# A new order for attention and projections in a one-core transformer layer: first tiles attended between quarters of the projections

## The reference

```python
h = rms_norm(x, g_attn); proj = h @ w_in        # aq 512, ak 64, av 64, iq 512, ik 64, iw 8, bq 512, bk 512, bv 512
# per-head RMSNorm (not for iq) and partial rotary on q and k heads
# group A: score = sum_h relu(iq_h . ik) * iw_h ; keep the top 128 keys of each query ; softmax attention, 8 heads, one k/v
# group B: 4 heads, two softmax maps each: (p1 - lam * p2) @ v, then RMSNorm over each head
# all masks are causal in chunks of 64 tokens
x = x + concat(y_a, y_b) @ w_o
h2 = rms_norm(x, g_ffn); logits = h2 @ w_router + b_router ; top 4 of 32 experts, softmax gates
x = x + sum over experts of gate * (clamped SwiGLU(h2 @ w_gu[e] + b_gu[e]) @ w_down[e] + b_down[e])
```

## Time and profile before

| | us |
|---|---|
| median of 3 runs (lowest, highest) | 1586.6 (1585.97, 1587.24) |
| the profiled execution, its own time | 1583.88 |
| its span from first to last instruction | 1582.1 |
| PE busy | 1475.2 (93%) |
| DVE busy | 1315.8 (83%) |
| ACT busy | 1104.1 (70%) |
| first expert matmul starts | 414.9 |
| PE busy from 500 us to the end | 1068.2 of 1082.1 |

### The profile page before, as it was taken

One profiled execution on the slowest core, in us unless ns is written; L12 is line 12 of the kernel. 1 busy time (PEld: TensorE's weight loads), 2 busy tenths in 40 slices (PEclk: granted clock), 3 DMA queues, 4 the chain that ended last, 5 costly groups with the idle time before them and its releaser, 6 DMA issues.

```text
span 1582.1 us, 18695 instructions
## 1 busy us (share of the span) xinstructions
PE 1475.2 (93%) x7098; PEld 1214.9 (77%) x7098; DVE 1315.8 (83%) x1274; ACT 1104.1 (70%) x1188; POOL 297.4 (19%) x160
## 2 busy tenths in 40 slices
PE   6888858998799999999999999999999999999996
PEld 5766646777577888888888888888888888888885
DVE  5668856554869999999999999999999999998994
ACT  5543454354567878888878878888878878888773
POOL 1644311001112111211112111211111111121101
PEclk9999968799799999999999999999999999999998
DMA  6311010115799999999999999999999999999991
GB/s 193 94 54 54 14 54 27 41 41 203 295 298 358 372 360 367 370 368 367 377 367 373 375 358 364 368 374 368 371 371 372 375 358 364 363 373 360 378 365 42
DMA packets 99244, 448.66 MB, mean 284 GB/s; under 512 B 18368, under 2 KB 19520, under 8 KB 66304
## 3 DMA queue, kind: packets, MB, share of 16 engines
q1 hardware_dynamic: 87264, 428.39, 70.2%
q0 software_dynamic: 9792, 18.90, 5.0%
q10 hardware_dynamic: 2080, 0.01, 0.1%
HBM read 440.95 MB, written 23.07 MB: 293 GB/s over the span
## 4 chain that ended last, share of the span: by engine, by line
PE 84%; DVE 9%; ACT 3%; issue 2%; DMA 0%; POOL 0%; SPq 0%; ACTq 0%; POOLq 0%; DVEq 0%
PE ps L1738 66%; PE ps L1530 2%; PE ps L1537 2%; PE ps L1532 2%; PE ps L1531 2%; PE ps L1748 2%; PE ps L1707 2%; PE ps L1699 2%; PE ps L1618 1%; DVE work L1240 1%; DVE top L1239 1%; DVE rp L1197 1%; DVE ss L1176 1%; PE ps L1648 1%; ACT W L875 1%
## 5 line engine op out<-in xcount | busy, mean ns | idle before, releaser
L653 DVE TENSOR_TENSOR whl<-wraw,whl 128x2048 fp32r<-128x2048 f32 x384 | 865.6, 2288 | 87.7 <-ACT whl L648 83.5
L648 ACT ACTIVATE whl<-wraw 128x2048 fp32r<-128x2048 f32 x384 | 733.1, 1918 | 206.6 <-PE ps L1738 206.4
L1738 PE MATMUL ps<-whl,xT 128*128 128x512 f32 x3120 | 732.2, 392 | 3.0 <-DVE xT L1438 1.7
L1738 PEld LDWEIGHTS ps<-whl,xT 128*128 128x128 f32 x3120 | 582.5, 188 | 124.0 <-issue 2.4
L1738 PE MATMUL ps<-whl,aT 128*128 128x512 f32 x1488 | 346.7, 392 | 0.0
L1738 PEld LDWEIGHTS ps<-whl,aT 128*128 128x128 f32 x1488 | 276.9, 188 | 57.1 <-DVE whl L653 0.3
L821 POOL DMA_INDIRECT out_dram<-ysb,idx x32 | 99.7, 3116 | 451.7 <-ACT ysb L1079 451.7
L812 POOL DMA_INDIRECT xg<-h_rows,idx x32 | 89.7, 2803 | 473.9 <-DVE idx L1426 470.8
L1530 PE MATMUL ps<-W,HT 128*128 128x512 f32 (+1 forms) x184 | 72.0, 392 | 1.7 <-DVE HT L1152 1.7
L1531 PE MATMUL ps<-W,HT 128*128 128x512 f32 (+1 forms) x184 | 70.0, 381 | 0.0
L1532 PE MATMUL ps<-W,HT 128*128 128x512 f32 (+1 forms) x184 | 69.7, 379 | 0.0
(11 more groups left out here) (233 smaller groups left out, 1452.2 us busy)
## 6 DMA issues: line engine op xcount, KB each, us to landing
wraw<-in_w_gu_dram SPq DMA_DIRECT2D x256, 1024.0 KB, 8.1
wraw<-in_w_down_dram SPq DMA_DIRECT2D x128, 1024.0 KB, 7.2
WR<-in_w_in_dram SPq DMA_DIRECT2D x20, 512.0 KB, 3.6
WR<-in_w_o_dram SPq DMA_DIRECT2D x8, 512.0 KB, 3.7
xs<-in_x_dram SPq DMA_DIRECT2D x4, 512.0 KB, 5.9
WR<-in_x_dram SPq DMA_DIRECT2D x4, 512.0 KB, 4.4
out_dram<-WR SPq DMA_DIRECT2D x4, 512.0 KB, 2.7
h_rows<-WR SPq DMA_DIRECT2D x4, 512.0 KB, 2.9
```

The lines of the kernel that those rows point to most:

```text
L648: act.activation(whl[:, n % HL, 0, :], wraw[n % RAW], ACT.Copy).then_inc(chunk_hi, 1)
L653: eng.tensor_tensor(whl[:, n % HL, 1, :], wraw[n % RAW], whl[:, n % HL, 0, :].bitcast(F32), ALU.subtract).then_inc(chunk_lo, 1)
L1738: ins = pe.matmul(bank, a[x_][j], w[:, b, j, 512 * q:512 * q + 512], start=c == NG and j == 0 and n == 0, stop=last and j == nj - 1 and n ...
```

## The change

The chunks are reordered to iq, kvi, aq, bq, bk, bv. A projection becomes four steps of two 128-row blocks (`PARTS`), and between them stand index scores (from stage 8 on, one a quarter), search rounds, and `ATTEND_AT[s]` units of attention. Units are renumbered by `unit(n)`: 0 to 7 are A of tile 0, 8 to 15 A of tile 1, 16 to 23 B of tile 0, 24 to 31 B of tile 1, then tiles 2 and 3 as before. 24 units fall into stages 14 to 22 (`ATTEND_AT`). Heads of bk are split and turned one stage later than others. w_o's splits stand one to a unit at 24 to 31; tile 3's 16 search rounds at units 32 to 47. The table `LATE` places the rest: output projections at units 37 to 44, 46 to 53, 55 to 62, and from 69; routers at 48, 57, 66 and 80 (before: output projections at 21, 37, 53, 69, and routers at 32, 48, 64, 80, each t at 16 units from the last).

The router's product goes to a transpose bank instead of ACC, so `out_proj` waits for `x1_ok` instead of the logits. A results of tiles 0 and 1 have buffers of their own (`yA`), B results of tile 1 use bank OA and another half of y, `work` and `maskA` are packed, and the waits follow the new order. With the last score, the list ends

```diff
 CHUNKS = [("iq", [(O_IQ, 512)]), ("kvi", [(O_IK, 72), (O_AK, 128)]), ("aq", [(O_AQ, 512)]),
-          ("bv", [(O_BV, 512)]), ("bq", [(O_BQ, 512)]), ("bk", [(O_BK, 512)])]
+          ("bq", [(O_BQ, 512)]), ("bk", [(O_BK, 512)]), ("bv", [(O_BV, 512)])]
-AHEAD = 5
+PARTS = 4
+ATTEND_AT = {14: 4, 15: 4, 16: 3, 17: 3, 18: 2, 20: 2, 21: 3, 22: 3}
...
+def unit(n):
+
+    if n < 16:
+        return n // 8, 8 + n % 8
+    if n < 32:
+        return (n - 16) // 8, n % 8
+    return n // 16, n % 16
...
+LATE = {11: [("mix_a", 0)], 19: [("mix_a", 1)],
+        34: [("mix_b", 0)], 35: [("mix_norm", 0)], 36: [("mix_b", 1), ("turn_y", 0)], 38: [("mix_norm", 1)],
+        43: [("mix_b", 2)], 45: [("mix_norm", 2), ("turn_y", 1)], 51: [("mix_a", 2)], 54: [("turn_y", 2)],
+        59: [("mix_b", 3)], 61: [("mix_norm", 3)], 67: [("mix_a", 3)], 68: [("turn_y", 3)]}
+for _t, _n in enumerate((37, 46, 55, 69)):
+    for _k in range(KD):
+        LATE.setdefault(_n + _k, []).append(("out_proj", _t, _k))
+    for _d, _kind in ((8, "post"), (9, "turn_x1"), (9, "post_mean"), (10, "post_norm"), (11, "route")):
+        LATE.setdefault(_n + _d, []).append((_kind, _t))
...
     def attend(n):
...
-            if t >= 1 and j == 7:
+            if t >= 1 and n in (8, 16 * t + 7):
                 while search and search[0][1] <= t:
                     plan.append(search.pop(0))
                 plan.append(("mask", t))
             plan.append(("score", n))
-            if t >= 1:
-                next_search(n >= 22 and n % 16 >= 6)
-        if pieces and n % 2:
+        if n >= 24 and pieces:
             plan.append(pieces.pop(0))
         if product_of(n - 1) and product_of(n - 1)[0] == "B":
             plan.append(("combine", product_of(n - 1)))
+        if n >= 32:
+            next_search(1)
...
+        plan.extend(LATE.get(n, []))
...
-        if s < n_items:
-            plan.append(("proj", s))
-        if s >= 10:
-            for _ in range(4):
-                if scores:
-                    plan.append(scores.pop(0))
-            if s < n_items:
-                next_search(3)
-        if s >= n_items:
-
-            for _ in range(AHEAD):
+        fill = ATTEND_AT.get(s, 0)
+        for q in range(PARTS):
+            if s < n_items:
+                plan.append(("proj", s, q))
+            if s >= first_kv + 5 and scores and ("turn_heads", first_kv + scores[0][1]) in plan:
+                plan.append(scores.pop(0))
+            if q < fill:
                 attend(attended.pop(0))
+            if s < n_items and q < (3 if s < 16 else 2):
+                next_search(1)
...
@@ SP
-            sp.wait_ge(values_ok, HB + HA)
+            sp.wait_ge(values_ok, values_no("B", 0, HB - 1))
             sp.dma_start(GF, bc(g_ffn)).then_inc(gf_in, 16)
...
@@ DVE, mix_a
-                    dve.wait_ge(values_ok, (HB + HA) * (t + 1))
+                    dve.wait_ge(values_ok, values_no("A", t, HA - 1))
...
@@ DVE, route
-                    dve.wait_ge(logit_ps, t + 1)
-                    dve.scalar_tensor_tensor(out=lg[:, t, :], in0=ps[:, ACC, 0:E], scalar=tss[:, 2:3], in1=brt,
-                                             op0=ALU.mult, op1=ALU.add).then_inc(logit_ok, 1)
-                    dve.wait_ge(logit_ok, t + 1)
+                    dve.wait_ge(turned, through(st))
+                    g = TURN[st]
+                    dve.scalar_tensor_tensor(out=lg[:, t, :], in0=tbank(g)[:, 0:E], scalar=tss[:, 2:3], in1=brt,
+                                             op0=ALU.mult, op1=ALU.add).then_inc(turn_read[g % 2], 1)
...
@@ PE, out_proj and route
-                        if t >= 1:
-                            pe.wait_ge(logit_ok, t)
+                        after(pe, x1_ok, t)
...
+                    g = TURN[st]
+                    wait_bank(pe, g)
                     for k in range(KD):
-                        ins = pe.matmul(ps[:, ACC, 0:E], x1T[:, k, :], wrt[:, k, :], start=(k == 0),
+                        ins = pe.matmul(tbank(g)[:, 0:E], x1T[:, k, :], wrt[:, k, :], start=(k == 0),
                                         stop=(k == KD - 1))
-                    ins.then_inc(logit_ps, 1)
+                    ins.then_inc(turned, 1)
```

More of the change, by code:

```diff
@@ L77, in keys_of, with product_of @@
     return P * (t + 1)
+def unit(n):
[4 more added lines that the diff above has]
+    return n // 16, n % 16
+UNITS = 16 * T
+NO = {unit(n): n for n in range(UNITS)}
+def product_of(n):
+    if not 0 <= n < UNITS:
+        return None
+    t, j = unit(n)
+    if j < 8:
+        return ("B", t, j // 2) if j % 2 else None
+    return ("A", t, j - 8)
+LATE = {11: [("mix_a", 0)], 19: [("mix_a", 1)],
[7 more added lines that the diff above has]
+        LATE.setdefault(_n + _d, []).append((_kind, _t))
 def make_plan():
@@ L93, in next_search @@
                 plan.append(search.pop(0))
[L97 to L108, removed]
     def attend(n):
-        if n == len(units) + 5:
+        if n == UNITS + 5:
             plan.append(("biases",))
-        if n < len(units):
-            t, j = units[n]
-            if t >= 1 and j == 7:
+        if n < UNITS:
+            t, j = unit(n)
+            if t >= 1 and n in (8, 16 * t + 7):
                 while search and search[0][1] <= t:
@@ L129, in attend @@
             plan.append(("values", product_of(n - 3)))
[L130 to L139, removed]
+        plan.extend(LATE.get(n, []))
+    attended = list(range(max(LATE) + 1))
     n_items = len(ITEMS)
+    first_kv = ITEM_NO[(CH["kvi"], 0)]
     for s in range(n_items + 3):
@@ L199 @@
 PROD = number(("turn_p",))
+COMBO = number(("combine",))
+REL_PRODS = 2 * HA + HB
 HEADED = [u for u in range(len(ITEMS)) if has_heads(u)]
@@ L585, in combo_no, with values_no, pv_bank @@
         def combo_no(pr):
-            return HB * pr[1] + pr[2] + 1
+            return COMBO[("combine", pr)] + 1
+        def values_no(which, t, h):
+            return PROD[("turn_p", (which, t, h))] + 1
+        def pv_bank(which, t):
+            return OA if which == "A" or t == 1 else OB
         def is0(r):
@@ L690, in _ @@
                 if t >= 1:
-                    sp.wait_ge(logit_ps, t)
+                    sp.wait_ge(turned, through(("route", t - 1)))
                 if t == T - 1:
@@ L1222, in _ @@
                     v, w = SCORE[st], keys_of(t)
-                    dst = work[:, t - 1, 0:w]
+                    dst = work[t]
                     dve.wait_ge(score_read, v + 1)
@@ L1547, in _ @@
                 elif kind == "proj":
-                    u = st[1]
+                    _, u, part = st
                     c, t = ITEMS[u]
-                    if u == 0:
+                    if u == 0 and part == 0:
                         wait_turns(pe, KD)
-                    if u >= 2:
+                    if u >= 2 and part == 0:
                         pe.wait_ge(raw_ok, u - 1)
                     dst = ps[:, ACC + u % 2, 0:WIDTH[c]]
-                    for k in range(KD):
+                    for k in range(KD // PARTS * part, KD // PARTS * (part + 1)):
                         if k % 2 == 0:
@@ L1578, in _ @@
                     n, v = st[1], SCORE[st]
-                    t, j = n // 16, n % 16
+                    t, j = unit(n)
                     w = keys_of(t)
-                    if j == 0:
-                        wait_turns(pe, through(("turn_heads", ITEM_NO[(WO - 1, t)])))
+                    if j % 8 == 0:
+                        wait_turns(pe, through(("turn_heads", ITEM_NO[(CH["bk" if j == 0 else "aq"], t)])))
                     pe.wait_ge(score_read, v - 1)
@@ L1594, in _ @@
                             pe.wait_ge(mask_ok, t)
-                        pe.matmul(dst, identb, maskA[:, t, 0:w], start=False, stop=False)
+                        pe.matmul(dst, identb, maskA[t], start=False, stop=False)
                     pe.matmul(dst, q, keys[1], start=False, stop=True).then_inc(score_ps, 1)
```

143 lines of the change are left out of this document (90 added, 53 removed).

## The result

The changed kernel takes 1599.09 us (median of 4 runs, 1596.39 to 1599.65) against 1586.92 us (4 runs, 1585.97 to 1589.15) for the kernel before beside it: ratio 1.0065, 95% interval 1.0048 to 1.0083. It is slower, by 0.65%; forecast were 1573 us and a range of 1556 to 1589.

The account below looks back on a forecast made before the run. DVE was taken to bound the projections with head work and tile 2, PE the bv projections and tile 3. Last maximum -16.6 us plus tail +3.0 gave -13.6, so 1573 us, range 1556 to 1589.

Parts of the forecast that it names:

- Stages 14 to 18: Projections 14 to 18 with 16 attention units between quarters: DVE bounds, 53.2 us, the units otherwise hidden behind DVE.
- To stage 10: Projections before stage 10, with tile 1's index scores: half of 3.9 us of DVE score passes hidden; group 10 starts near 80.3.
- Stages 10 to 13: Projections 10 to 13 with head work, searches and index scores: DVE bounds, 48.9 us; PE needs about 8 a group.
- Stages 19 to 22: The bv projections, without head work of their own: PE bounds, 38.7 us, starting up to 4 us before DVE ends group 18.
- Units 24 to 31: Attention after the projections with one w_o split per unit: 3.6 us each, 29 us, bounds 23 and 31.
- Tile 2: Units 32 to 47 carrying 16 search rounds: DVE work of 43.9 us plus waits makes 55 us, ending at 303.
- Tile 3: Last attention tile, PE-bound, with 14 output-projection slices instead of 8: 51 us, last maximum at 354 against 370.62.
- The tail: After the last score: router 2 behind the last value product +1.9, post 2 and turn_x1 2 +1.1; +3.0 us, bounds 0 and 5.
- The expert stage: Untouched stage after the front stage, starting at 414.9 us before: as long as before, front-stage savings coming through whole.
- rival 3: Moved work costs what it saves, all bounds at bad ends, projections ending at 223: about -1 us, 1586; chance 0.16.
- Rival 2: PE's clock falls to half under the projections, stages 10 to 17, so PE bounds: +32 us, 1605; chance 0.10.
- rival 1: PE, not DVE, bounds tile 2; searches hide and dense matmuls get full clock: units 32 to 63 91.5 us, 1558.6; chance 0.18.

Follow-up runs that it names:

- `units_behind`: Changed kernel with no attention units between projection quarters, all 64 after the last projection; 1593.65 us, ratio 1.0035 to the kernel before.
- `old_chunks`: Changed kernel, all units after the projections, chunks in old order (bv before bq, bk), bk heads not delayed; 1590.71 us, ratio 1.0024 to the kernel before.
- `old_chunks_tail`: `old_chunks` with first three output projections at units 37, 45, 53 and second turn of y at 53; 1592.70 us, ratio 1.0027 to the kernel before.

## Why the prediction was wrong

The failed step is "Stages 14 to 18", and in it the sentence that the A units "are otherwise hidden behind DVE". The sum put DVE's work at 53.2 us where 43.5 were measured, in part because its ropes were fast; with the right load the same rule would have given less still. What failed is that the stretch was taken for the sum of the busiest engine. It was 68.2 us, +15.0, and taking 8.8 us of DVE's work away changed nothing.

Step by step, with what each did to the error of 22.7 us at the first expert matmul:

- *To stage 10*: 84.4 instead of 80.3 us, +4.1. The forecast counted half of DVE's score passes; in the trace PE waits 2.9 us in stages 8 and 9 for ACT's copies of index scores, DVE's rope takes 2.45 us at 76.97 (0.28 before, at 75.67), and the clock from 65 to 84.4 us is 0.91 instead of 1.00.
- *Stages 10 to 13*: 48.1 for 48.9, DVE busy 42.6. Near, with DVE the fullest engine as forecast: -0.8.
- *Stages 14 to 18*: +15.0, above.
- *Stages 19 to 22*: 38.1 for 38.7, PE-bound (35.5), right. The 2 us by which I let them overlap group 18 weren't there: together +1.5, so the last projection came at 238.8 instead of 219.
- *Units 24 to 31*: 28.5 for 29. Right.
- *Tile 2*: 53.0 for 55, the number near, the reason wrong: without the 16 searches it is still 49.3, so they cost 3.7 us. -2.0.
- *Tile 3*: 54.4 for 51, +3.4. PE was busy in 51.1 of it at a clock of 0.94; the sum had left it at the 1.00 of the earlier trace rows and took 2 us off for idle time taken back.
- *The tail*: +4.7 us for +3.0. Moving the router back gave 1 us by experiment.
- *The expert stage* "as long as before": it varies by up to 7 us between profiles (1167.2 to 1174.4), so the span of one execution against another is worse evidence than the last maximum.

On the rivals: rival 3 (the moved work costs what it saves) is nearest, and its terms fell past their bad ends: the projections ended at 239, not 223. Rival 2 came out slower, as the kernel did, but not by its mechanism: the clock over stages 14 to 18 was 0.90, and PE had 17 us of idle time there. Half clock appears in it behind the long waits, as a consequence: between 84 and 239 us PE waited 1.5 us or more nine times, and the clock was 0.50 for some 3 us behind each of the six waits of 3.05 to 3.94 us and behind none of the three of 1.99 to 2.48 (in the second profile it was behind the one of 2.35).

Of the signs that the prediction named, the clock gave no warning (0.92 from 90 to 180 us), but DVE was busy in 70.9 of those 90 us, 79% and not over 85, and PE did wait in the quarters for ACT's exponentials (the sign "it is wrong if"): 9.3 us in stages 14 to 18.

Three readings in the prediction were wrong from the start. The earlier trace rows don't show half clock "wherever PE pauses a lot": from 284.1 us PE is busy in 17.1 of 17.8 us at 0.58, so dense work alone didn't give full clock there, which also takes something from " agree" in rival 1. The "about 6.6 in 10" of rival 2 is 7.2 in the row (14.66 of 20.50 us). And not every rope beside a GpSimd split was slow before the change either: the one at 75.67 took 0.28 us, behind a scaling of 1.57 us beside the split that began at 73.34.

**Where the gain went.** The change reaches the 32nd unit 16.5 us earlier than before, which is what it has to give. But 8 slices of output projection (1.36 us each, 10.9) and the searches of tile 3 (3.7) left the stretch before it and stand after it. Units 32 to 63 take 107.4 us instead of 86.5: +20.9, of which these are 14.6, the turned tile 1.1 (the slices and the tile are estimates from their matmuls), and the remaining 5.2 I put down to the lower clock and PE's waits, which no run took apart. That alone is +4.4 at the last maximum. The forecast had seen this (+19.5) and counted on 36 us of lead, not 16.5. Of the lead that was missing, 15 us are the ring in stages 14 to 18. Undoing it in full (`units_behind`) gives back only 3.2 us, because the units then need 25 us of their own: no order that ran had 36 us of lead. The most was 23.0, in the profile of `old_chunks` (261.1 against 284.1), of its fastest run; with the same list up to there `old_chunks_tail` had 15.6. In the former the last maximum comes 4.4 us before that of the kernel before, and its tail of 49.1 us (366.2 to 415.3) against 44.3 takes it back. So in every profile what the new order gains in the middle is paid in full by units 32 to 63 and the tail.

## What to carry to other kernels

Interleaving two chains of work hides one under the other only if each engine's queue doesn't put a link of the one between two links of the other: look at the idle time of *all* engines in a stretch before taking the busiest one's sum for its length, and allow for a wait at each place where the lists couple. Test the load before trusting it: leave a part of the busiest engine's work out (here a fifth), and if the stretch stays as long, what sets it is not that engine's load. And follow what leaves a sparse stretch to where it is due next: here 14.6 us went from a stretch with idle engines to one that PE filled.

## What the runs showed of the hardware

- The clock of a sparse stretch differs between executions of the same list: 0.55 and 0.65 over the same 198 matmul records, 5.5 us apart; and behind the same wait of 2.35 us 0.50 in one profile of the changed kernel and 1.00 in the other, 1.6 us apart over the stage. How much of the spread of times comes from it wasn't measured: the three versions with all units behind the projections ran from 1581.5 to 1599.1 us, the kernel before from 1582.0 to 1592.9.
- A small VectorE scaling of 128x8 took 1.20 to 1.48 us beside a GpSimd weight split, and 0.17 with GpSimd idle, and then the rope that my sum had slow was fast (0.28). Who pays for the split depends on which instruction meets it.
- Behind the six waits of 3.05 to 3.94 us between 84 and 239 us PE ran at half clock for some 3 us; in the lap shown its projection matmuls then start 0.42 us apart instead of 0.23 (166.98 and 167.40, against 160.31 and 160.54). So such a wait cost more than its length.
